# Expert rows of a two-block network: gate, diagonal and add of a row move into the row's own turn

## The chip, the cores and the metric

The kernel runs on one core of a Trainium2 chip. The metric is the device time of one launch in microseconds (us); lower is better. A core has five engines with instruction streams of their own that meet only at semaphores: TensorE (PE), VectorE (DVE), ScalarE (ACT), GpSimd (POOL), and SyncE (SP), which here only issues DMAs. Each stream is executed in its written order, so an instruction that waits holds up all that is written behind it on its engine.

## The reference

All data are float32: 512 tokens, width 1024. A first block (two layers: short convolution or state-space mixer, each with a gated feed-forward) is followed by a hybrid layer (band attention beside a gated delta rule) and then by the part that this change is about, a product-key retrieval of single-neuron experts. For each block of 128 tokens:

```
top_s, pos = lax.top_k(cand_s, 16)            # 8 heads x 16 = 128 experts per token
gates = softmax(top_s)
u, vv = expert_down[experts], expert_up[experts]
act = gelu(sum_d u * h)                       # one dot product per token and expert
out = sum_k (gates * act) * vv                # weighted sum of 128 rows of 1024
```

Every token needs 128 rows of two tables, 4 KB each: with 512 tokens that is 537 MB.

## The kernel before

**Chunks and rows.** The tokens are worked in four chunks `c` of 128, one token per partition. A "row" `n` = 128c + s (s from 0 to 127) is the s-th expert of all 128 tokens of chunk c at once. POOL gathers it (`pool_gather`, L2173) with one indirect DMA: 1 MB, 2048 words a partition, first the down half and then the up half. `GG` is 1, so a group is one row. The gathers go into a ring of buffers: 7 slots for rows 0 to 255, 12 from row 256 on. A gather waits until the row that used its slot before has been added (L2178).

**The work on one row** is: a dot product of the down half with the token's vector on DVE (`dve_dots`, L2182); the gelu of the 128 dots on ACT (L2200); the product with the row's gate; and the add of the up half, weighted by the result. Three rows of four (and for n of 256 and more 15 of 16) are added by PE: ACT makes a 128x128 diagonal matrix of the weights (`act_diag`, L2206), and PE multiplies it with the up half in two matmuls into two PSUM banks (`pe_add`, L2218). The others are DVE's own (`own_add`, L2163): s at least 24 and s = 1 mod 4 while n is below 256, s = 9 mod 16 after that. DVE adds such a row with one multiply-add of 1024 columns (`dve_add`, L2249). PE and ACT skip it.

**What runs between the rows.** The order of each engine's stream is written out by hand in `pe_experts` (L2306), `act_experts` (L2323) and `dve_experts` (L2342), which all loop over the 512 rows. In each odd row, every engine also does one step of other work (`steps_of`, L2297): for chunks 0 and 1 a step of `main`, the whole hybrid layer of the second half of the tokens (normalisation, projections, attention, the delta rule with its inversion `pe_invert`/`dve_invert`, output, queries), and beside it steps of the top-16 search of the next chunk (`dve_topk`, all on DVE). The step of an odd row is the same step on all three engines. In the inversion, the products of PE's step are masked or subtracted by DVE in the same step, and PE's next step needs the result.

**The order inside a row's turn `g`, before:**

- DVE: dots(g); gate product (g-1); own add (g-1), if it is DVE's; if g is odd, the step.
- ACT: gelu(g); diagonal(g-1); if g is odd, the step.
- PE: if g is odd, the step; add(g-1).

So the weight of a row passes ACT, DVE, ACT and PE, and its gate, diagonal and add stand in the turn of the row after it. L numbers in the profile are mostly those of helpers (`Engine`, L137 to L217): L153 is a matmul, L158 a transpose, L164 an ACT operation, L187 the dot product, L170 a tensor-tensor operation on DVE, L182 a multiply-add on DVE, L216 a gather.

Of the kernel before, what the change touches and what calls it, by code (L numbers as in the profile page):

```python
# [5 lines left out]
ALU = mybir.AluOpType  # L6
ACT = mybir.ActivationFunctionType
# [13 lines left out]
GG = 1  # L21
# [205 lines left out]
def build(nc, t, out):  # L227
    ctx = ExitStack()
    with ctx:
# [891 lines left out]
        t_at = [0]  # L1121

        def room(n):
            a = t_at[0]
            t_at[0] += n
            assert t_at[0] <= WORDS - LOW, t_at[0]
            return tail[:, a:a + n]
# [20 lines left out]
        gates = [room(128) for _ in range(2)]  # L1148
        eidx = [room(128).bitcast(U32) for _ in range(2)]
        dots = [room(GG) for _ in range(8)]  # L1150
# [3 lines left out]
        d_nega = room(1)  # L1154
        sm = [room(4) for _ in range(4)]
        NRING = (WORDS - LOW - t_at[0]) // 2048
        RING = t_at[0]
        ring_mem = [room(2048) for _ in range(NRING)]
        T = tiles(over[:, 4096:6144], 8)
        Sb = [over[:, 6144 + 512 * i:6656 + 512 * i] for i in range(3)]  # L1160
# [28 lines left out]
        k_dve, k_gate, idx_ok, gate_ok = [signal(n) for n in ("ranked", "gate_exp", "experts_found", "gates")]  # L1189
        tk_pe, f_pe, f_g, f_add = [signal(n) for n in ("turned_h", "turned_x", "gate_row", "out_added")]  # L1190
        g_dot, g_gelu, g_act, g_diag, g_mm = [
            signal(n) for n in ("dots", "gelu", "gated", "diag", "expert_added")]
# [959 lines left out]
        GROUPS = 128 // GG  # L2152
# [37 lines left out]
                e.wait_ge(*g_in.at((c, GG * grp + i)))  # L2190
                e.ttr(s[:, 0:1024], s[:, 0:1024], htk[c % 2], d[:, i:i + 1]).then_inc(*g_dot.tick(n + i))

        def dve_gate(e, c, grp):
            n = 128 * c + GG * grp
            d = dots[(n // GG) % 8]
            e.wait_ge(*g_gelu.at(n))
            e.wait_ge(*gate_ok.at(c))
            e.tt(d, d, gates[c % 2][:, GG * grp:GG * grp + GG], ALU.mult).then_inc(*g_act.tick((c, grp)))

        def act_gelu(e, c, grp):  # L2200
            n = 128 * c + GG * grp
            d = dots[(n // GG) % 8]
            e.wait_ge(*g_dot.at(n + GG - 1))
            e.act(d, d, ACT.Gelu).then_inc(*g_gelu.tick(n))

        def act_diag(e, c, grp):  # L2206
            n = 128 * c + GG * grp
            d = dots[(n // GG) % 8]
            e.wait_ge(*g_act.at((c, grp)))
            for i in range(GG):  # L2210
                if own_add(n + i):
                    continue
                k = turn[n + i]
                if k >= 8:
                    e.wait_ge(*g_mm.at(by_pe[k - 8]))
                e.act(diag[k % 8], ident, ACT.Copy, scale=d[:, i:i + 1]).then_inc(*g_diag.tick(n + i))

        def pe_add(e, c, grp):  # L2218
            for i in range(GG):
                s_i = GG * grp + i  # L2220
                n = 128 * c + s_i
                if own_add(n):
                    continue
                if s_i == 0:
                    for u in range(2):
                        ps.claim(("acc", c, u), (u,))
                        e.wait_ge(*ps.vacant(("acc", c, u)))
                e.wait_ge(*g_in.at((c, s_i)))
                e.wait_ge(*g_diag.at(n))
                for u in range(2):  # L2230
                    ins = e.mm(ps["acc", c, u], diag[turn[n] % 8], SLOTS[slot_no[n]][:, 1024 + 512 * u:1536 + 512 * u],
                               s_i == 0, s_i == 127)
                ins.then_inc(*g_mm.tick(n))

        def pe_finish(e, c):
            for u in range(2):
                o = ps.claim(("gB", c, u), HB)
                e.wait_ge(*ps.vacant(("gB", c, u)))
                e.wait_ge(*der_ok.at((5, "post")))
                for k in range(4):  # L2240
                    ins = e.mm(o[:, part[k]], post(5, 4 * u + k).broadcast_to([128, 128]), ident)
                ins.then_inc(*f_pe.tick(("gB", c, u)))
                o = ps.claim(("xo", c, u), HB)
                e.wait_ge(*ps.vacant(("xo", c, u)))
                for k in range(4):
                    ins = e.tr(o[:, part[k]], xT[:, 4 * u + k, 128 * c:128 * c + 128], ident)
                ins.then_inc(*f_pe.tick(("xo", c, u)))
# [56 lines left out]
        ALL_GROUPS = [(c, grp) for c in range(4) for grp in range(GROUPS)]  # L2304

        def pe_experts(e):  # L2306
            main = pe_main(e, 1)
            before_rows(main, iter(()))
            for g, (c, grp) in enumerate(ALL_GROUPS):
                if grp == 0:  # L2310
                    ranks = iter(()) if c == 3 else wait_steps(32)
                    late = pe_tok(e, 3) if c == 2 else iter(())
                if grp % 2:
                    steps_of(c, grp // 2, main, ranks)
                    next(late, None)
                if g:
                    pe_add(e, *ALL_GROUPS[g - 1])
                if g and grp == 0:
                    pe_finish(e, c - 1)
            pe_add(e, *ALL_GROUPS[-1])  # L2320
            pe_finish(e, 3)

        def act_experts(e):  # L2323
            ranked = [act_topk(e, c) for c in range(4)]
            main = act_main(e, 1, ranked[2])
            before_rows(main, iter(()))
            drive(ranked[0])
            for g, (c, grp) in enumerate(ALL_GROUPS):
                if grp == 0:
                    ranks = iter(()) if c == 3 else ranked[c + 1]  # L2330
                    late = act_tok(e, 3) if c == 2 else iter(())
                act_gelu(e, c, grp)
                if g:
                    act_diag(e, *ALL_GROUPS[g - 1])
                if c and grp == 8:
                    store(e, c - 1)
                if grp % 2:
                    steps_of(c, grp // 2, main, ranks)
                    next(late, None)
            act_diag(e, *ALL_GROUPS[-1])  # L2340

        def dve_experts(e, ranks):  # L2342
            ranked = [ranks] + [dve_topk(e, c) for c in range(1, 4)]
            main = dve_main(e, 1, ranked[2])
            before_rows(main, ranks)
            drive(ranks)
            for g, (c, grp) in enumerate(ALL_GROUPS):
                if grp == 0:
                    ranks = iter(()) if c == 3 else ranked[c + 1]
                    late = wait_steps(3) if c == 2 else iter(())  # L2350
                dve_dots(e, c, grp)
                if g:
                    dve_gate(e, *ALL_GROUPS[g - 1])
                    dve_add(e, *ALL_GROUPS[g - 1])
                if c and grp == 1:
                    dve_finish(e, c - 1)
                if grp % 2:
                    steps_of(c, grp // 2, main, ranks)
                    next(late, None)
            dve_gate(e, *ALL_GROUPS[-1])  # L2360
            dve_add(e, *ALL_GROUPS[-1])
            dve_finish(e, 3)

# [230 lines left out]
```

## Time and profile before

| | |
|---|---|
| time, median of 3 runs | 3613.56 us (3610.62 to 3616.09) |
| time of the profiled execution | 3612.0 us |
| its span in the profile | 3610.2 us |
| busy: PE / weight load / DVE / ACT / POOL | 3070.5 / 2105.5 / 2132.0 / 1193.7 / 603.5 us |
| first gather starts | 2100.9 us |
| gathers | 512, in 73728 packets, 536.90 MB |
| chain that ended last | PE 60%, DVE 16%, DMA 13%, ACT 5%, issue 4% |

The span is from the first instruction to the end of the last. An engine's busy time is the union of its instructions. The granted TensorE clock (PEclk) is a share of full speed. A row of the timeline has the start in us from the span's start, the duration in us, engine, line, operation, tiles (written<-read), shape, how many instructions were merged, and in brackets the idle time before it with what ended it. Rows of the kernel can be told by counting the dot products (L187 with 128x1024): the 91st is that of row 90.

### The profile page before, as it was taken

What the parts mean: (1) busy time and instruction counts of PE and PEld (TensorE: products, weight loads), DVE (VectorE), ACT (ScalarE), POOL (GpSimd) and SP (SyncE); (2) the same over time, 40 slices, a digit from 0 to 9 for tenths busy, and PEclk for the clock granted to TensorE, in tenths of its full rate; (3) what the DMA queues carried; (4) which work ended last, traced back from release to release, by engine and by line L of the source; (5) the groups of instructions that cost most, each with busy time, mean ns of one, the idle gap of its engine ahead of it and who ended that gap; (6) DMA issues with size and microseconds to landing.
All of it is one profiled execution on the core that took longest, in us unless ns stands there. A gap on an engine that the chain in (4) does not pass through costs nothing.

```text
span 3610.2 us, 34684 instructions
## 1 busy us (share of the span) xinstructions
PE 3070.5 (85%) x12138; PEld 2105.5 (58%) x12138; DVE 2132.0 (59%) x4304; ACT 1193.7 (33%) x2363; POOL 603.5 (17%) x540
## 2 busy tenths in 40 slices
PE   5989999798777989998998887988889677777777
PEld 4868888587565768886777753655457222222222
DVE  6655443676455454433353589876656978755555
ACT  2233222443444432222562345651222211211111
POOL 0000000000000000000000022323343454444442
PEclk9999999899888999999999998999999799999999
DMA  5534444242111324442311286988999899999997
GB/s 219 188 125 140 140 141 141 77 142 89 47 36 41 117 94 140 140 144 72 129 60 58 97 312 233 353 352 299 362 397 381 313 409 421 421 422 421 421 422 326
DMA packets 147548, 797.83 MB, mean 221 GB/s; under 512 B 16304, under 2 KB 18480, under 8 KB 81712
## 3 DMA queue, kind: packets, MB, share of 16 engines
q0 software_dynamic: 73728, 536.90, 37.2%
q1 hardware_dynamic: 69840, 251.69, 21.3%
q10 hardware_dynamic: 3808, 7.02, 0.5%
q8 instruction: 98, 1.61, 0.2%
q14 instruction: 74, 0.61, 0.0%
HBM read 793.46 MB, written 2.10 MB: 220 GB/s over the span
## 4 chain that ended last, share of the span: by engine, by line
PE 60%; DVE 16%; DMA 13%; ACT 5%; issue 4%; POOL 0%; DVEq 0%; SPq 0%; ACTq 0%
PE psum L153 60%; DMA tail<-in_experts,tail 13%; DVE tail L187 5%; ACT arena L164 3%; DVE tail L170 2%; DVE arena L182 2%; ACT L164 2%; DVE tail L182 1%; DVE tail L193 1%; DVE tail L190 1%; DVE region L170 1%; PE psum L158 1%; ACT region L164 1%; DVE tail L196 1%; DVE tail L205 1%
## 5 line engine op out<-in xcount | busy, mean ns | idle before, releaser
L153 PE MATMUL psum<-tail,arena 128*128 128x512 f32 (+2 forms) x3652 | 1322.9, 510 | 317.1 <-ACT arena L164 293.5
L153 PE MATMUL psum<-rounded,rounded 128*128 128x512 f32 x5496 | 1293.0, 396 | 40.9 <-DVE rounded L182 28.2
L153 PEld LDWEIGHTS psum<-tail,arena 128*128 128x128 f32 x3652 | 687.9, 199 | 903.0 <-issue 847.2
L153 PEld LDWEIGHTS psum<-rounded,rounded 128*128 128x128 f32 x5496 | 1036.2, 190 | 280.7 <-issue 56.1
L216 POOL DMA_INDIRECT tail<-in_experts,tail x512 | 583.4, 1139 | 1840.2 <-DVE tail L199 949.5
L187 DVE CUSTOM_DVE_ANT_0 tail<-tail 128x1024 f32<-128x1024 f32 x512 | 626.0, 1223 | 322.6 <-DMA tail<-in_experts,tail 320.2
L170 DVE TENSOR_TENSOR rounded<-arena,rounded 128x1024 fp32r<-128x1024 f32 (+2 forms) x285 | 316.3, 1110 | 346.7 <-ACT rounded L164 346.6
L164 ACT ACTIVATE tail<-tail 128x1 f32<-128x1 f32 (+2 forms) x544 | 115.4, 213 | 1032.5 <-DVE tail L187 878.0
L164 ACT ACTIVATE rounded<-arena 128x1024 fp32r<-128x1024 f32 (+2 forms) x317 | 291.9, 939 | 446.3 <-DVE arena L170 238.9
L153 PE MATMUL psum<-arena 128*128 128x1 f32 (+3 forms) x792 | 197.6, 374 | 75.1 <-ACT arena L164 45.2
L164 ACT ACTIVATE arena<-psum 128x256 f32<-128x256 f32 (+2 forms) x210 | 97.5, 480 | 440.3 <-PE psum L153 439.9
L164 ACT ACT_TABLE_LOAD x186 | 238.6, 1283 | 11.8 <-PE psum L153 6.4
L182 DVE SCALAR_TENSOR_TENSOR arena<-arena 128x512 f32<-128x512 f32 (+1 forms) x294 | 212.1, 724 | 21.8 <-ACT arena L164 10.9
L170 POOL TENSOR_TENSOR region<-region 128x256 f32<-128x256 f32 x24 | 19.9, 830 | 1131.0 <-DVE region L170 1131.0
L153 PEld LDWEIGHTS psum<-arena 128*128 128x128 f32 x792 | 127.3, 205 | 126.1 <-issue 81.0
L164 ACT ACTIVATE arena<-arena,tail 128x128 f32<-128x128 f32 x446 | 172.8, 388 | 0.8 <-issue 0.2
L170 DVE TENSOR_TENSOR tail<-tail 128x1 f32<-128x1 f32 (+4 forms) x555 | 134.4, 243 | 30.8 <-ACT tail L164 24.0
L153 PE MATMUL psum<-tail 128*128 128x128 f32 (+4 forms) x888 | 136.9, 300 | 16.8 <-DVE tail L182 14.7
L170 DVE TENSOR_TENSOR arena<-psum,arena 128x512 f32<-128x512 f32 (+1 forms) x88 | 41.5, 475 | 168.3 <-PE psum L153 168.0
L153 PEld LDWEIGHTS psum<-tail 128*128 128x128 f32 (+2 forms) x888 | 107.7, 185 | 52.5 <-issue 28.7
L182 DVE SCALAR_TENSOR_TENSOR arena<-psum,arena 128x511 f32<-128x511 f32 (+3 forms) x112 | 79.8, 712 | 77.0 <-ACT arena L164 44.0
L164 ACT ACTIVATE arena<-arena 128x512 f32<-128x512 f32 (+3 forms) x138 | 80.7, 598 | 89.9 <-DVE arena L170 29.3
(82 smaller groups left out, 1537.8 us busy)
## 6 DMA issues: line engine op xcount, KB each, us to landing
arena<-in_ada SPq DMA_DIRECT2D x136, 512.0 KB, 3.8
arena<-in_fin SPq DMA_DIRECT2D x88, 512.0 KB, 4.3
arena<-in_win SPq DMA_DIRECT2D x56, 512.0 KB, 3.3
arena<-in_fout SPq DMA_DIRECT2D x32, 512.0 KB, 4.1
arena<-in_mxbc SPq DMA_DIRECT2D x32, 512.0 KB, 4.1
arena<-in_pq SPq DMA_DIRECT2D x32, 512.0 KB, 5.2
arena<-in_ain SPq DMA_DIRECT2D x24, 512.0 KB, 4.7
arena<-in_mz SPq DMA_DIRECT2D x16, 512.0 KB, 3.6
```

The source lines that it names most:

```text
L153: return self.e.matmul(o, a, b, start=start, stop=stop, skip_group_check=skip)
L158: return self.e.transpose(o, a, ident)
L164: return self.e.activation(o, a, func, bias=bias, scale=scale)
L170: return self.e.tensor_tensor(o, a, b, op)
L182: return self.e.scalar_tensor_tensor(out=o, in0=a, scalar=s, in1=b, op0=op0, op1=op1)
L187: return self.e.tensor_tensor_reduce(o, a, b, 1.0, 0.0, ALU.mult, ALU.add, total)
L190: return Unissued() if self.e is None else self.e.max(o, a)
L193: return Unissued() if self.e is None else self.e.max_index(o, m, a)
L196: return Unissued() if self.e is None else self.e.match_replace(o, m, a, -3.0e38)
L205: return Unissued() if self.e is None else self.e.tensor_reduce(o, a, AX_X, op)
L216: return self.e.indirect_dma_start(out=o, out_offset=None, in_=table, in_offset=bass.IndirectOffsetOnAxis(ap=rows, axis=0))
```

## The change

The gate product moves from DVE to ACT, as a copy with a per-partition scale, right behind the gelu of the same row; ACT makes the diagonal in the same turn; PE adds the row in the same turn. DVE's own add stays one turn later. The order in turn `g` becomes:

- DVE: dots(g); own add (g-1); if g is odd, the step.
- ACT: gelu(g); gate product(g); diagonal(g); if g is odd, the step.
- PE: if g is odd, the step; add(g).

The closing work of a chunk on PE (`pe_finish`) moves to the end of turn 127 of that chunk. `RING = t_at[0]`, which nothing reads, is deleted.

```diff
-        def dve_gate(e, c, grp):
-            n = 128 * c + GG * grp
-            d = dots[(n // GG) % 8]
+        def act_gate(e, c, grp):
+            n = 128 * c + grp
+            d = dots[n % 8]
+            e.wait_ge(*g_dot.at(n))
+            e.act(d, d, ACT.Gelu).then_inc(*g_gelu.tick(n))
+            e.wait_ge(*gate_ok.at(c))
             e.wait_ge(*g_gelu.at(n))
-            e.wait_ge(*gate_ok.at(c))
-            e.tt(d, d, gates[c % 2][:, GG * grp:GG * grp + GG], ALU.mult).then_inc(*g_act.tick((c, grp)))
-
-        def act_gelu(e, c, grp):
-            ...
-            e.wait_ge(*g_dot.at(n + GG - 1))
-            e.act(d, d, ACT.Gelu).then_inc(*g_gelu.tick(n))
+            e.act(d, d, ACT.Copy, scale=gates[c % 2][:, grp:grp + 1]).then_inc(*g_act.tick((c, grp)))
@@ pe_experts
-                if g:
-                    pe_add(e, *ALL_GROUPS[g - 1])
-                if g and grp == 0:
-                    pe_finish(e, c - 1)
-            pe_add(e, *ALL_GROUPS[-1])
-            pe_finish(e, 3)
+                pe_add(e, c, grp)
+                if grp == GROUPS - 1:
+                    pe_finish(e, c)
@@ act_experts
-                act_gelu(e, c, grp)
-                if g:
-                    act_diag(e, *ALL_GROUPS[g - 1])
+                act_gate(e, c, grp)
+                act_diag(e, c, grp)
...
-            act_diag(e, *ALL_GROUPS[-1])
@@ dve_experts
                 if g:
-                    dve_gate(e, *ALL_GROUPS[g - 1])
                     dve_add(e, *ALL_GROUPS[g - 1])
...
-            dve_gate(e, *ALL_GROUPS[-1])
```

## Rows read from the trace of the kernel before

**Rows 1.** Windows: us, busy us (instructions) per engine, PEclk, DMA share, GB/s.
```profile
2293.00:2366.00 73.00, 72.74 (x280) 50.10 (x279) 60.27 (x155) 50.65 (x99) 21.78 (x22) 1.00 0.97 374
2398.00:2525.00 127.00, 100.90 (x487) 67.72 (x488) 87.05 (x169) 26.74 (x73) 41.23 (x34) 0.92 0.80 293
...
2688.00:2807.00 119.00, 118.20 (x503) 84.27 (x501) 79.41 (x218) 29.19 (x105) 43.82 (x37) 1.00 0.96 380
2807.00:2893.00 86.00, 49.09 (x74) 17.74 (x73) 81.95 (x198) 18.77 (x54) 36.12 (x25) 0.76 0.82 312
2950.00:3590.00 640.00, 479.97 (x1009) 177.09 (x1009) 411.29 (x997) 125.61 (x497) 270.93 (x252) 0.97 1.01 420
```

**Rows 2.** Waits from 2100 to 2900: us in total, times, longest us.
```profile
POOL tail L216 <- PE psum L153: 472.3, 165, 9.6
...
DVE tail L187 <- DMA tail<-in_experts,tail: 76.9, 58, 3.9
```

**Rows 3.** Waits from 2398 to 2525 (inversion of the delta rule).
```profile
DVE tail L170 <- PE psum L153: 31.6, 14, 4.8
PE psum L153 <- ACT arena L164: 26.4, 15, 4.0
```

**Rows 4.** Timeline of PE in the inversion, rows 88 to 92.
```profile
2442.59 1.89 PE L153 MATMUL psum<-tail,arena 128*128 128x512 f32 x4
2444.32 1.95 PE L153 MATMUL psum<-tail 128*128 128x128 f32 x16
2447.90 1.96 PE L153 MATMUL psum<-tail,arena 128*128 128x512 f32 x4 [1.63 <-ACT arena L164]
2450.24 1.96 PE L153 MATMUL psum<-tail,arena 128*128 128x512 f32 x4 [0.39 <-ACT arena L164]
2452.04 3.73 PE L153 MATMUL psum<-tail 128*128 128x128 f32 x32
```

**Rows 5.** Timeline of DVE in the same stretch, rows 90 to 94.
```profile
2443.40 1.22 DVE L187 CUSTOM_DVE_ANT_0 tail<-tail 128x1024 f32<-128x1024 f32 x1
...
2444.54 0.15 DVE L170 TENSOR_TENSOR tail<-tail 128x1 f32<-128x1 f32 x1
...
2447.15 1.28 DVE L170 TENSOR_TENSOR tail<-psum,tail 128x512 f32<-128x512 f32 x2
2448.35 1.21 DVE L187 CUSTOM_DVE_ANT_0 tail<-tail 128x1024 f32<-128x1024 f32 x1
...
2457.01 1.22 DVE L187 CUSTOM_DVE_ANT_0 tail<-tail 128x1024 f32<-128x1024 f32 x1
```

**Rows 6.** Timeline of ACT in the same stretch, rows 90 and 91.
```profile
2444.66 0.20 ACT L164 ACTIVATE tail<-tail 128x1 f32<-128x1 f32 x1 [6.23 <-DVE tail L187]
...
2447.36 0.39 ACT L164 ACTIVATE arena<-arena,tail 128x128 f32<-128x128 f32 x1
```

**Rows 7.** Timeline of ACT in the projections, row 51.
```profile
2303.70 0.36 ACT L164 ACTIVATE arena<-psum 128x256 f32<-128x256 f32 x1
...
2305.38 0.42 ACT L164 ACTIVATE tail<-tail 128x256 f32<-128x256 f32 x1
2305.82 0.42 ACT L164 ACTIVATE arena<-tail 128x256 f32<-128x256 f32 x1
```

**Rows 8.** Timelines of PE and ACT around row 70.
```profile
2365.68 7.49 PE L153 MATMUL psum<-tail,arena 128*128 128x256 f32 x30
2374.69 1.96 PE L153 MATMUL psum<-tail,arena 128*128 128x512 f32 x4 [1.51 <-ACT arena L164]
2378.50 3.68 PE L153 MATMUL psum<-tail,arena 128*128 128x512 f32 x12 [1.85 <-ACT arena L164]
...
2373.71 0.29 ACT L164 ACTIVATE tail<-tail 128x1 f32<-128x1 f32 x2
```

**Rows 9.** Timelines of ACT and PE at the end of the kernel.
```profile
3599.06 0.20 ACT L164 ACTIVATE tail<-tail 128x1 f32<-128x1 f32 x1 [1.97 <-DVE tail L187]
...
3603.21 1.05 PE L153 MATMUL psum<-arena 128*128 128x128 f32 x8
```

More of the change, by code:

```diff
@@ L1156, in build @@
         NRING = (WORDS - LOW - t_at[0]) // 2048
-        RING = t_at[0]
         ring_mem = [room(2048) for _ in range(NRING)]
@@ L2191, in dve_dots @@
                 e.ttr(s[:, 0:1024], s[:, 0:1024], htk[c % 2], d[:, i:i + 1]).then_inc(*g_dot.tick(n + i))
-        def dve_gate(e, c, grp):
-            n = 128 * c + GG * grp
-            d = dots[(n // GG) % 8]
-            e.wait_ge(*g_gelu.at(n))
-            e.wait_ge(*gate_ok.at(c))
-            e.tt(d, d, gates[c % 2][:, GG * grp:GG * grp + GG], ALU.mult).then_inc(*g_act.tick((c, grp)))
-        def act_gelu(e, c, grp):
-            n = 128 * c + GG * grp
-            d = dots[(n // GG) % 8]
-            e.wait_ge(*g_dot.at(n + GG - 1))
-            e.act(d, d, ACT.Gelu).then_inc(*g_gelu.tick(n))
+        def act_gate(e, c, grp):
[4 more added lines that the diff above has]
+            e.wait_ge(*gate_ok.at(c))
+            e.wait_ge(*g_gelu.at(n))
+            e.act(d, d, ACT.Copy, scale=gates[c % 2][:, grp:grp + 1]).then_inc(*g_act.tick((c, grp)))
         def act_diag(e, c, grp):
```

## The prediction, made blind

> **What bounds the kernel now.** I read the windows of the expert phase first. From 2950 to 3590 the DMA engines are taken whole: share 1.01, 420 GB/s, while PE is busy for 480 us of 640 and ACT for 126 [rows 1]. A gather is 1 MB, so a row costs 2.5 us there whatever the engines do. The end of the kernel is therefore the moment at which this DMA-bound stretch starts, plus a fixed amount of gathering; time is won or lost before it, from the first gather at 2100.9 to about 2893. There the reader is to see a different limit in each stretch. From 2293 to 2366 and from 2688 to 2807 PE is busy nearly throughout (72.7 of 73 us, 118.2 of 119). From 2807 to 2893, and from 2107 to 2202 in the same way, DVE is (82.0 of 86: the top-16 search). From 2398 to 2525, the inversion, nobody is: PE 101 and DVE 87 of 127 us, and the DMA engines carry only 293 GB/s [rows 1]. The waits say what this stretch is: DVE waits 31.6 us for PE, and PE 26.4 us for ACT's diagonal [rows 3]. It is a loop between engines, bound by latency. So I read its timeline next, engine by engine [rows 4 to 6].
>
> **One turn of that loop, before.** Its length is four rows, 2443.40 to 2457.01 = 13.61 us [rows 5]. Call the rows 90 to 93; row 89 and row 93 are DVE's own, which PE skips. After the step of row 89, PE does add(88) at 2442.59, whose diagonal is long there, and at once the step of row 91 at 2444.32, 16 matmul records for two token chunks [rows 4]. Meanwhile DVE is at dots(90), own add and dots(91), and when it comes to its own part of step 91 at 2447.15, PE's products lie ready and it waits for nothing [rows 5]. Only then does PE do add(90), 2447.90, and add(91), 2450.24, and the step of row 93 at 2452.04 [rows 4].
>
> **The change, part by part.**
>
> *Gate product to ACT.* It is a dependent ACT operation on one column. Its duration I take from the gelu, 0.20 us [rows 6]. An ACT operation that needs the one before starts 0.02 us after that one's end (2305.38 + 0.42, next at 2305.82) [rows 7]; so gelu to product is 0.23, and product to diagonal again 0.23: the diagonal starts 0.46 after the gelu. Before, the diagonal (of the row before) started 0.10 after the gelu (2447.36, behind a gelu of 0.20 whose record ends at 2447.46). ACT's chain grows by 0.36 per row. Bounds: 0.2, if the two pipeline as before, and 0.8, if each step takes the 0.44 of the wide pair [rows 7]. The Trainium skill ("ScalarE: Activation LUTs", Rules for kernel authors) wants a multiply on VectorE and budgets about 0.3 us for each ACTIVATE. No row shows a one-column product on ACT; by that figure the chain would be 0.6 and not 0.46, some 4 us more in the sum below.
>
> *Gate product off DVE.* It lasts 0.15 but starts before the dot product's end (2444.54, against 2443.40 + 1.22) and sticks out by 0.07 [rows 5]. That counts where DVE is the bound, in some 50 rows: 2 to 3 us, I take -2. Elsewhere it is worth nothing. It also removes a wait of DVE for ACT's gelu, but behind it DVE next needs ACT's output or a slot, so nothing again.
>
> *Add in its own turn, on PE.* This is the term that decides. The same three adds per four rows are done, but PE's step of row g now stands behind add(g-1) and no more behind add(g-2). For g = 1 mod 4 little changes: step 93 stood behind add(91), which needs the turn of dots(92) anyway; now it stands behind add(92), which needs the same dots. For g = 3 mod 4 it does: row 89 is DVE's own, so step 91 could start with add(88) done; now it must wait for row 90's whole chain. Worked out: gelu(90) is at 2444.66; the diagonal at 2445.12; diagonal to matmul is 0.54 (2447.36 to 2447.90) [rows 4, 6], so add(90) at 2445.66; an add holds PE for 1.73 (2442.59 to 2444.32), so step 91 at 2447.39 and not 2444.32. The first half of its products is there 1.05 us later, and DVE's part starts about 2448.5 and not 2447.15; its second half waits for PE's as well, so dots(92) comes at 2450.05 and not 2448.35: +1.70. Behind that, gelu(92) comes 1.26 after the start of its dots (as 2443.40 to 2444.66), add(92) 1.00 after that, and step 93 another 1.80 later (2450.24 to 2452.04), at 2454.1 and not 2452.04. One turn of the loop becomes 2.06 us longer, 15%. Hidden before was PE's step 91, by DVE's two dot products and own add; its cover is gone.
>
> The rows 90 to 113 hold six such turns: 12.4 us. Two more lie ahead of them in the stretch, and two behind it up to 2558, where the delta rule's advance runs; their steps are of other lengths, some half as long, and I take the 1.70 of the first part alone for each: 6.8. Both terms together lie between 12 (the first part without the second, in fewer turns) and 24.
>
> *A long ACT step.* Around row 70, ACT is in table loads until 2373.71 [rows 8]. Before, PE does step 71 in the meantime (until 2365.68 + 7.49 = 2373.17), then waits for diagonal(70) until 2374.69 and for diagonal(71) until 2378.50; 1.8 behind that, at 2380.3, step 73 begins [rows 8]. Now step 71 stands behind add(70), whose own chain ends at 2374.9: it starts near 2376.6 and ends, with 3.7 of matmuls (a step of 16 records there, an estimate from 7.49 for 30), near 2380.3. Add(71) takes it to 2382.1, and add(72) needs a gelu behind ACT's step 71, which itself now has its product later: step 73 begins near 2384.8. PE is busy for long behind that, so it stays: +4.5. Bounds 0 and 7.
>
> *Projections, 2293 to 2366.* ACT's evacuation of PE's product (2303.70) stands behind the diagonal [rows 7], and DVE waits for it. That loop takes 0.36 more in each of 11 steps: 4. PE is busy here too, so the cost lies between 0 (PE alone decides) and 8. I take 4, since both loops have the same length.
>
> *PE-bound 2688 to 2807.* PE runs behind ACT's diagonals, so whether it adds g or g-1 first changes nothing: 0, or 2 at the start.
>
> *DMA-bound rest.* A slot is freed about one row (2.5 us) earlier, but the DMA engines are full: 0. *The end.* Before, add(510) and add(511) both come behind gelu(511) at 3599.06, and the closing matmuls start at 3603.21 [rows 9]. Now only add(511) does: one add less (1.73) and 0.36 more: -1.4.
>
> **Sum:** 12.4 + 6.8 + 4.5 + 4 - 2 - 1.4 = 24.3 us. On the profiled execution's 3612.0 that is 3636.3, and 1.5 more for the median of the runs shown: 3637. The bounds of the terms give 3620 to 3662.
>
> **Rivals.**
>
> *The ring pays back (faster).* Of the time from 2100 to 2900 POOL spends 472 us in 165 waits for a slot that PE frees [rows 2]. Every slot now comes back a row earlier, with 7 slots in all. If the gathers are what holds DVE back there, its 76.9 us of waits for landings shrink; two thirds gone and no loss elsewhere gives 3612 - 51 = 3561. For it: POOL's waits are the longest in the profile. Against it: DVE waits for landings in 58 places only, 1.3 us each [rows 2], and in the inversion what it waits for is PE [rows 3]; from 2688 to 2807 PE is the busy one anyway [rows 1]. The Trainium skill ("Perfetto Trace Analysis", Identifying Performance Opportunities) says that the same gap repeating can mean too few buffers. POOL's gaps repeat so, and by that rule this rival would win; but what the rule speaks of is the engine that should be saturated, and in the inversion that is none.
>
> *A draw.* The slots won shorten the waits for landings around 2581 to 2807 by about the 24 us that the loops lose: 3613.
>
> *Every step pays.* If PE's order costs 2.06 per four rows in all of rows 35 to 207, the PE-bound stretches too, since PE then waits at each step for ACT behind DVE: 43 times 2.06 = 89, so 3612 + 89 - 3 = 3698. Against it: there the diagonals are several us ahead of PE.
>
> **Chances.** Forecast 0.62, the ring 0.13, a draw 0.11, every step 0.14. A difference of under 0.2% (7 us) can't be told from none. Faster is the ring, 0.13; the same is the draw, 0.11; slower is the rest, 0.76. The predicted time is 3637. The range reaches down to the draw and up half way to the third rival: 3609 to 3668.
>
> **What would show it.** Right: between 2398 and 2558 four rows take about 15.7 us and not 13.6; PE's waits for ACT's diagonal there grow, and stand in front of the short step; DVE's masking behind dots of g = 3 mod 4 gets a wait for PE of about 1.3 us. The gate shows as a second one-column ACT operation 0.23 behind the gelu. The stretch at 420 GB/s keeps its rate and starts some 26 us later. Wrong: if the inversion keeps its 13.6 us, PE's step doesn't hang on the row; if waits for landings fall by tens of us, the ring decides; and if the PE-bound stretches grow, the ACT chain does.

## The result, and the profile after

The changed kernel takes 3643.96 us (median of 4 runs, 3642.29 to 3646.46), the kernel before 3612.09 in the same comparison (4 runs, 3608.34 to 3616.09): a ratio of 1.0087, with a 95% interval of 1.0070 to 1.0104. Forecast were 3637 and slower. The profiled execution took 3642.49, its span is 3640.6.

First the windows of the changed kernel. The window of the inversion begins 17 us later than in [rows 1] and is 20 us longer; the columns are the same.

```profile
2415.00:2562.00 147.00, 103.31 (x482) 68.59 (x480) 82.77 (x130) 37.58 (x101) 43.41 (x33) 0.89 0.65 237
2980.00:3620.00 640.00, 483.45 (x1012) 177.63 (x1011) 394.77 (x747) 226.35 (x752) 265.03 (x254) 0.97 1.01 421
```

The last stretch is as full as before: 421 GB/s and 1.01 against 420 and 1.01 [rows 1]. Only ACT has more in it, 226 us for 126, and that costs nothing there. The inversion is emptier: PE is busy for 103 of 147 us, where it was 101 of 127, the DMA engines carry 237 GB/s for 293, and PE's granted clock is 0.89 for 0.92. The waits say who waits for whom (changed kernel, 2100 to 2900: us in total, times, longest):

```profile
POOL tail L216 <- PE psum L153: 400.1, 156, 10.3
...
PE psum L153 <- ACT arena L164: 145.7, 58, 7.5
...
DVE tail L170 <- PE psum L153: 64.8, 30, 5.4
DVE tail L187 <- DMA tail<-in_experts,tail: 45.9, 29, 5.6
```

DVE waits less for landings (45.9 us for 76.9 [rows 2]), and this is what the rival of the ring had foreseen in kind. But it waits 64.8 us for PE, and PE 145.7 for ACT's diagonal. The same two lines before:

```profile
PE psum L153 <- ACT arena L164: 117.1, 54, 7.1
...
DVE tail L170 <- PE psum L153: 34.2, 17, 4.8
```

Both grew by about 30 us, and the time, 3643.96, lies above the first two rivals (3561 and 3613). Where the waits for landings fell is the next thing to look at. None of it is in rows 90 to 113 of the inversion, where DVE waits for no landing before or after; nearly all is in rows 128 to 207. There (first the kernel before, 2558 to 2811, then the changed one, 2598 to 2849):

```profile
DVE tail L187 <- DMA tail<-in_experts,tail: 68.7, 51, 3.9
...
DVE arena L182 <- PE psum L153: 5.5, 4, 2.4
```

```profile
DVE tail L187 <- DMA tail<-in_experts,tail: 37.4, 26, 5.2
DVE arena L182 <- PE psum L153: 32.1, 8, 4.1
```

DVE waits 31 us less for landings and 27 us more for PE's products, and the rows take 1.3 us less. PE is busy for over 90% of this stretch in both kernels (232.7 of 253 us, 230.0 of 251), so the wait changed its name and little else.

Now the turn of the inversion that the prediction worked out, engine by engine, in the changed kernel (start us, duration us, then the instruction). DVE, rows 90 to 98:

```profile
2459.08 1.22 DVE L187 CUSTOM_DVE_ANT_0 tail<-tail 128x1024 f32<-128x1024 f32 x1
...
2464.40 0.69 DVE L170 TENSOR_TENSOR tail<-psum,tail 128x512 f32<-128x512 f32 x1 [1.75 <-PE psum L153]
...
2465.90 1.22 DVE L187 CUSTOM_DVE_ANT_0 tail<-tail 128x1024 f32<-128x1024 f32 x1
...
2472.05 1.28 DVE L170 TENSOR_TENSOR tail<-tail,psum 128x512 f32<-128x512 f32 x2 [3.78 <-PE psum L153]
...
2475.03 1.22 DVE L187 CUSTOM_DVE_ANT_0 tail<-tail 128x1024 f32<-128x1024 f32 x1
...
2492.37 1.22 DVE L187 CUSTOM_DVE_ANT_0 tail<-tail 128x1024 f32<-128x1024 f32 x1
```

ACT, row 90:

```profile
2460.40 0.53 ACT L164 ACTIVATE tail<-tail 128x1 f32<-128x1 f32 x2 [5.14 <-DVE tail L187]
2460.96 0.40 ACT L164 ACTIVATE arena<-arena,tail 128x128 f32<-128x128 f32 x1
```

PE, rows 90 to 94:

```profile
2461.51 1.96 PE L153 MATMUL psum<-tail,arena 128*128 128x512 f32 x4 [3.07 <-ACT arena L164]
2463.31 1.95 PE L153 MATMUL psum<-tail 128*128 128x128 f32 x16
2465.09 1.88 PE L153 MATMUL psum<-tail,arena 128*128 128x512 f32 x4
2468.27 1.96 PE L153 MATMUL psum<-tail,arena 128*128 128x512 f32 x4 [1.29 <-ACT arena L164]
2470.06 3.73 PE L153 MATMUL psum<-tail 128*128 128x128 f32 x32
2477.47 3.35 PE L153 MATMUL psum<-tail,arena 128*128 128x512 f32 x4 [3.67 <-ACT arena L164]
```

The reader is to see the order that was foreseen. Before, step 91 (16 records) stood at 0.92 behind the dot product of row 90 (2444.32 against 2443.40 [rows 4, 5]), and DVE found its products ready. Now it stands at 4.23 behind it (2463.31 against 2459.08), with PE idle for 3.07 us in front of add(90), and DVE waits 1.75 us where it waited for nothing. The turn is 2459.08 to 2475.03 = 15.95 us, where it was 13.61. The next turn, to 2492.37, is 17.34: its add at 2477.47 takes 3.35 us and not 1.96, and the whole difference is there (1.39 us).

**Where the time went.** Each row of the experts has one dot product on DVE, and they are counted off in the traces. The table gives the time between the starts of the dot products of the rows named (us, one profiled execution of each kernel; "start" is when row 0's begins). The lower lines are the experiments of the next section; each is introduced there.

```
kernel              start |  0-44  44-70  70-90 90-114 114-128 128-208 208-256 256-end | row 0 to end
before             2107.3 | 166.0   92.8   77.4   81.4    33.6   252.3   142.0   657.5 | 1502.9
before, again      2114.6 | 166.2   92.6   80.8   81.4    33.6   252.7   143.1   657.7 | 1508.1
changed            2114.9 | 161.0   95.2   88.1  102.5    36.8   251.0   137.1   654.2 | 1525.7
changed, again     2107.3 | 160.8   95.2   88.0  104.3    38.4   251.1   136.3   654.6 | 1528.7
e1_pe_late         2115.0 | 161.9   95.2   64.8   66.5    34.2   246.1   137.0   654.4 | 1460.0
e2_own_even        2103.5 | 165.4   95.7   78.8   80.5    33.6   245.2   141.8   654.6 | 1495.7
e3_fill            2115.0 | 161.3   95.2   87.8   94.6    36.7   251.9   137.6   653.5 | 1518.6
e4_gate_only       2109.0 | 160.7   95.5   83.3   80.8    32.8   253.3   142.2   655.7 | 1504.5
e5_defer2          2115.0 | 162.5   95.1   76.1   80.7    31.9   250.2   136.7   654.2 | 1487.6
e6_defer0          2107.1 | 163.0   95.3   74.5   78.9    32.5   248.6   136.7   654.5 | 1483.9
e7_two_late        2109.1 | 171.7  109.2   65.4   65.0    36.4   257.6   138.2   653.6 | 1497.0
e8_ring6           2103.1 | 169.0   93.8   81.5   79.3    35.6   261.4   148.0   659.1 | 1527.8
```

Of the changed kernel's loss, 21.1 us lie in rows 90 to 113 and 3.2 in the 14 behind them; rows 70 to 89 lose 10.7, rows 44 to 69 lose 2.4; rows 0 to 43 give 5.0 back, rows 128 to 207 1.3, rows 208 to 255 4.9, the rest 3.3.

### The profile page after: what moved, and what is told of

The parts are those of the page before. It is cut to its first block, busy times and chain, and to the rows that moved or that the text cites. A ratio compares the mean times of both kernels' runs of the same rounds, so it can differ in the third digit from the quotient of the medians.

```text
span 3640.6 us, 34668 instructions
## 1 busy us (share of the span) xinstructions
PE 3077.4 (85%) x12138; PEld 2110.5 (58%) x12138; DVE 2091.3 (57%) x3792; ACT 1392.2 (38%) x2875; POOL 594.1 (16%) x540
## 4 chain that ended last, share of the span: by engine, by line
PE 59%; DMA 16%; DVE 15%; ACT 6%; issue 3%; POOL 0%; DVEq 0%; SPq 0%; ACTq 0%; POOLq 0%
PE psum L153 58%; DMA tail<-in_experts,tail 15%; DVE tail L187 4%; ACT arena L164 2%; DVE arena L182 2%; ACT L164 2%; DVE tail L170 1%; ACT tail L164 1%; DVE tail L182 1%; DVE tail L193 1%; DVE tail L190 1%; DVE region L170 1%; PE psum L158 1%; ACT region L164 1%; DVE tail L196 1%
## 5 line engine op out<-in xcount | busy, mean ns | idle before, releaser
L153 PE MATMUL psum<-tail,arena 128*128 128x256 f32 (+2 forms) x3652 | 1324.7, 511 | 357.0 <-ACT arena L164 333.4
L216 POOL DMA_INDIRECT tail<-in_experts,tail x512 | 574.0, 1121 | 1872.3 <-DVE tail L199 949.5
L164 ACT ACTIVATE tail<-tail 128x1 f32<-128x1 f32 (+1 forms) x1056 | 266.1, 252 | 817.9 <-DVE tail L187 796.8
L182 DVE SCALAR_TENSOR_TENSOR arena<-arena 128x512 f32<-128x512 f32 (+1 forms) x294 | 212.3, 724 | 21.8 <-ACT arena L164 10.8
L153 PE MATMUL psum<-region 128*64 128x128 f32 (+2 forms) x560 | 85.5, 387 | 33.9 <-DVE region L170 32.9
```

The source lines that it names most:

```text
L153: return self.e.matmul(o, a, b, start=start, stop=stop, skip_group_check=skip)
L164: return self.e.activation(o, a, func, bias=bias, scale=scale)
L182: return self.e.scalar_tensor_tensor(out=o, in0=a, scalar=s, in1=b, op0=op0, op1=op1)
L216: return self.e.indirect_dma_start(out=o, out_offset=None, in_=table, in_offset=bass.IndirectOffsetOnAxis(ap=rows, axis=0))
```

## Experiments

The theory (1): PE's step of row g now stands behind add(g-1) and so behind the newest dot product; DVE's work no longer covers it. Rivals: (A) ACT's longer chain costs it, whatever PE's order; (B) a part of the loss lies ahead of row 0 and belongs to the code; (C) to add in the row's own turn costs at every step; the price of a slot is measured at the end. Beside them stands theory (2): the fall of PE's clock in the inversion is a price of its own. Edits are against the changed kernel where nothing else is said.

**PE's add one turn later again.** ACT still makes gelu, product and diagonal in the row's own turn.

```diff
-                pe_add(e, c, grp)
-                if grp == GROUPS - 1:
-                    pe_finish(e, c)
+                if g:
+                    pe_add(e, *ALL_GROUPS[g - 1])
+                if g and grp == 0:
+                    pe_finish(e, c - 1)
+            pe_add(e, *ALL_GROUPS[-1])
+            pe_finish(e, 3)
```

> The changed kernel, except that PE adds row g-1 in turn g, as before the change. ACT keeps gelu, gate product and diagonal in the row's own turn. Theory 1 (PE's step lost its cover: it now stands behind the add of the row just before it): the inversion goes back to about 13.6 us for four rows, without PE's 3.1 to 3.7 us waits ahead of those adds; what is left of the change is a gain of some 4 to 6 us on DVE's search stretches: 3605 to 3613, ratio to before 0.998 to 1.000. Rival A (ACT's chain of 0.56 us from gelu to diagonal, where it was 0.10, is what costs): stays at 3630 to 3644, since that chain is kept. Rival B (7.6 us of the difference lie ahead of the first row and belong to the code): they show again at row 0.

Measured: 3570.08 (5 runs, 3567.15 to 3578.18), 0.9883 of the kernel before (0.9867 to 0.9899; its median 3612.46). The order on PE is what costs, as theory 1 has it, and rival A falls. But the size was missed by some 35 us: this kernel is not level with the one before but 1.2% faster, the fastest of this study. The expectation had the inversion back at 13.6 us a turn; it went to 11.47. Its PE in the same stretch, rows 90 to 94, whose dots(90) starts at 2448.45 and dots(94) at 2459.92:

```profile
2448.76 1.95 PE L153 MATMUL psum<-tail 128*128 128x128 f32 x16
2450.88 1.96 PE L153 MATMUL psum<-tail,arena 128*128 128x512 f32 x4 [0.17 <-ACT arena L164]
2453.16 1.96 PE L153 MATMUL psum<-tail,arena 128*128 128x512 f32 x4 [0.32 <-ACT arena L164]
2454.95 3.73 PE L153 MATMUL psum<-tail 128*128 128x128 f32 x32
2458.52 1.88 PE L153 MATMUL psum<-tail,arena 128*128 128x512 f32 x4
```

Step 91 is back ahead of add(90), and add(90), which waited 1.63 us for its diagonal before [rows 4], waits 0.17. Before, diagonal(90) stood on ACT behind gelu(91), hence behind dots(91). Made at once, it lies ready, and step 93 starts 6.50 us behind dots(90) instead of 8.64 (2452.04 less 2443.40 [rows 4, 5]). The turn is 11.47 us. So the change joins a gain with a larger loss. Of DVE's waits from 2100 to 2900, that for landings is longer here than in the kernel before (76.9 us [rows 2]), though the kernel is the fastest:

```profile
DVE tail L187 <- DMA tail<-in_experts,tail: 91.4, 68, 5.9
```

**The gate's product alone.** The edit of e1, and on ACT also the diagonal one turn later: only the product has moved, from DVE to ACT.

```diff
-                act_diag(e, c, grp)
+                if g:
+                    act_diag(e, *ALL_GROUPS[g - 1])
+            act_diag(e, *ALL_GROUPS[-1])
```

> The gate product moves to ACT, but ACT's diagonal and PE's add stay one turn later as in the kernel before. Theory 1: no step loses its cover; DVE is rid of 512 small operations: 3604 to 3611 (ratio 0.998 to 1.000), about as the kernel with only PE's add late. Rival A (the second ACT operation itself costs): some us slower than before, the more in the projections (2293 to 2366), 3620 or more.

Measured: 3614.95, a ratio of 1.0007 (0.9997 to 1.0017): no difference. It was expected at 3604 to 3611, a little faster, with 3620 or more as the rival (A); it falls between the two. It gains 5.3 us in rows 0 to 43, where DVE is the bound, and loses 2.7 in rows 44 to 69. This and the kernel of e1 differ only in the turn in which ACT makes the diagonal: 3614.95 - 3570.08 = 45 us. And e1 and the changed kernel differ only in the turn of PE's add: 3643.96 - 3570.08 = 74 us the other way. 3 - 45 + 74 is the whole result. (These are differences of medians of several batches; in the profiled executions, from row 0 to the end, the two are 44.5 and 65.7 us.) The 45 us do not come from the inversion alone: rows 70 to 89 give 18.5 of them, rows 90 to 113 14.3, rows 128 to 255 12.4.

**DVE's own rows laid on even turns.** The rows that DVE adds itself become n = 2 mod 4 instead of 1 mod 4, so PE has no row to add just ahead of its step of n = 3 mod 4.

```diff
-            return s >= 24 and (s % 4 == 1 if n < 256 else s % 16 == 9)
+            return s >= 24 and (s % 4 == 2 if n < 256 else s % 16 == 10)
```

> The changed kernel, except that DVE's own rows are s = 2 mod 4 (and 10 mod 16) and not 1 and 9. The work is the same. Theory 1: PE has now nothing to do between add(1) and the step of row 3, so this step no longer stands behind the row just before it; its cover is back though each add stays in its own turn: four rows of the inversion take 13.6 to 14.1 us, in all 3606 to 3620. Rival A (ACT's longer chain): nothing changes, 3640. Rival C (adding in the row's own turn costs at every step): the inversion stays above 16 us, 3635 or more.

Measured: 3607.85, 0.9987 (0.9979 to 0.9996), 36 us under the changed kernel, with its ACT chain kept and every add still in its own turn. So neither (A) nor (C) costs what the changed kernel loses. Rows 90 to 113 take 80.5. Its turn is 13.82 us (dots(90) 2443.40, dots(94) 2457.22). In the turn behind it PE idles 1.31 and 1.52 us ahead of its two adds, not 3.67 as in the changed kernel:

```profile
2457.53 1.95 PE L153 MATMUL psum<-tail 128*128 128x128 f32 x16
2460.79 1.96 PE L153 MATMUL psum<-tail,arena 128*128 128x512 f32 x4 [1.31 <-ACT arena L164]
2464.27 1.96 PE L153 MATMUL psum<-tail,arena 128*128 128x512 f32 x4 [1.52 <-ACT arena L164]
```

The cost sits where an add of a new row stands ahead of a step, as theory 1 says.

**Which of the two steps.** Two kernels put one of the two adds of a turn of four behind the step that follows it: e5 with k = 2 (the add of n = 2 mod 4 goes behind step n = 3 mod 4), e6 with k = 0 (that of n = 0 mod 4 behind step n = 1 mod 4). The edit is shown once for both.

```diff
+                if grp % 4 == k + 1: pe_add(e, c, grp - 1)     # behind the step
...
-                pe_add(e, c, grp)
+                if grp % 4 != k: pe_add(e, c, grp)
```

> The changed kernel, but PE's adds of rows n = 2 mod 4 come behind the step of the next row, so that only this step (rows n = 3 mod 4) is freed from the row just before it; the step of rows n = 1 mod 4 still stands behind add(n-1). By my prediction this is the whole loss: the inversion goes to about 14 us for four rows, rows 90 to 114 to 83 us (working from the timeline of the kernel with late adds: dots, gelu, gate and diagonal put step 93 2.4 us later than its 11.5 us loop has it). Rival (each kind of step costs half): 88 to 94.

> The opposite half: PE's adds of rows n = 0 mod 4 come behind the next step (n = 1 mod 4), the step of rows n = 3 mod 4 stays behind add(n-1). If a half can be taken alone, as I work it out from the timeline of the kernel with late adds, the loop takes about 12.8 us and rows 90 to 114 take 77 us. By my prediction, which gave all the loss to the other kind of step, it stays near 100.

Measured: e5 3602.18, 0.9966 (0.9949 to 0.9982); e6 3592.86, 0.9960 (0.9946 to 0.9973). Rows 90 to 113 take 102.5 with neither step freed, 80.7 with step 3 alone, 78.9 with step 1 alone and 66.5 with both (e1). The prediction said that step 3 is what the change costs and that step 1 stands as before. e5 bears this out: with step 3 free and step 1 still behind the newest row the stretch is back at 80.7, where it was 81.4. e6 does not: by the prediction it was to stay near 100, and it went to 78.9. Each step costs something behind a new row, and more when the other one stands there too: step 3 costs 12.4 us with step 1 free (66.5 to 78.9) and 21.8 with step 1 bound (80.7 to 102.5); slow adds, the subject of the next experiment, are a part of both. What is true of the prediction's claim is that the kernel before had paid for step 1 already, since its diagonal was made so late, and not for step 3. (The medians of e5 and e6 lie 9 us apart, but the intervals of their ratios overlap.) DVE in e5, rows 90 to 94:

```profile
2448.64 1.22 DVE L187 CUSTOM_DVE_ANT_0 tail<-tail 128x1024 f32<-128x1024 f32 x1
...
2452.12 1.28 DVE L170 TENSOR_TENSOR tail<-psum,tail 128x512 f32<-128x512 f32 x2
...
2459.50 1.29 DVE L170 TENSOR_TENSOR tail<-tail,psum 128x512 f32<-128x512 f32 x2 [3.78 <-PE psum L153]
...
2462.49 1.22 DVE L187 CUSTOM_DVE_ANT_0 tail<-tail 128x1024 f32<-128x1024 f32 x1
```

The masking of step 91 waits for nothing again, that of step 93 for 3.78 us, and the turn is 13.85. The kernel before waited 3.17 us at that place, and e1 takes it down to 1.40: its adds of rows 90 and 91 hardly wait for their diagonals (0.17 and 0.32 us, above). DVE, first the kernel before, then e1:

```profile
2454.02 1.28 DVE L170 TENSOR_TENSOR tail<-tail,psum 128x512 f32<-128x512 f32 x2 [3.17 <-PE psum L153]
```

```profile
2456.93 1.29 DVE L170 TENSOR_TENSOR tail<-tail,psum 128x512 f32<-128x512 f32 x2 [1.40 <-PE psum L153]
```

**Filling PE's idle time.** The slow add of the changed kernel at 2477.47 can be laid beside the clock that PE was granted (window 2477 to 2479; the columns are those of the windows, so the clock is the 0.50):

```profile
2477.00:2479.00 2.00, 1.53 (x2) 0.84 (x3) 1.60 (x3) 0.65 (x3) 1.27 (x1) 0.50 0.05 20
```

It is half of full speed, the lower of the two levels; over the turn before, 2459 to 2475, it is 1.00. The experiment asks whether PE's activity decides it. In rows 88 to 115, at n = 2 mod 4, PE does two more matmuls with a zero stationary matrix before it waits for the diagonal. They add zero to the sums; only PE's activity changes.

```diff
+            if 88 <= n < 116 and n % 4 == 2:
+                for u in range(2):
+                    e.mm(ps["acc", c, u], zero, SLOTS[...][:, 1024+512*u:1536+512*u], False, False)
             e.wait_ge(*g_diag.at(n))
```

> The changed kernel, and for rows 88 to 115 with n = 2 mod 4 PE does two more matmuls of 128x512 with a zero matrix (they add nothing) before it waits for the diagonal, in time in which it stands idle. Theory 2 (in the inversion the adds of 3.0 to 3.8 us behind an idle time of 3.67 us are slow because the granted clock fell; others take 1.96): the idle time is cut to about 1.9 us, the adds take 1.96, a turn falls from 17.3-17.9 to about 15.9 us, 6 to 10 us less in all: 3634 to 3638. Rival (these adds are slow because of the data or the memory they read): they stay at 3.3, and the time at 3644.

Measured: 3628.94, 1.0046 (1.0033 to 1.0058). Rows 90 to 113 go from 102.5 to 94.6. The add at the place of the slow one, PE of this kernel:

```profile
2477.45 1.99 PE L153 MATMUL psum<-tail,arena 128*128 128x512 f32 x4 [1.86 <-ACT arena L164]
2479.27 1.95 PE L153 MATMUL psum<-tail 128*128 128x128 f32 x16
```

It takes 1.99 us again and not 3.35, though PE was given more to do. Of the five such adds (rows 94 to 110) four take 1.99; one, that of row 98, still takes 3.21. The median fell by 15 us, more than the 6 to 10 that were expected. In the profiled executions, from row 0 to the end, it is 7.1 us, and this is the number that belongs to the filled stretch. Turn by turn, from row 90 on (us between the starts of the dot products of rows 90, 94, ... 114, read off the traces):

```
before       13.61  14.67  14.62  13.62  13.61  11.23
changed      15.95  17.34  18.85  17.62  17.65  15.08
e3_fill      15.89  15.89  17.57  15.89  15.89  13.52
e1_pe_late   11.47  11.48  11.48  11.48  11.48   9.09
changed, 2nd 15.95  18.97  17.62  17.65  17.51  16.56
e8_ring6     13.61  13.61  13.62  13.61  13.61  11.23
```

The reader is to see a base and something on top. Without the slow adds the six turns would be 5 x 13.61 + 11.23 = 79.3 us before and 5 x 15.89 + 13.52 = 93.0 after: 13.7 us for the wait. The slow adds put 2.1 on top before (two turns of six) and 9.5 after (five of six): 7.4 us for the clock. The two make the 21.1. The last line, the kernel before with one slot less (below), happens to have no slow add here, and it takes those 79.3 us. How often the clock falls is not fixed: in its second profile the changed kernel takes 104.3 us and not 102.5, so the clock's part is 7 to 9 us.

**Both kernels again.** No edit; one more profile of each.

> The kernel before, unchanged, for a second profile. In the first pair of profiles the changed kernel reaches row 0 7.6 us later than the kernel before, though all code ahead is the same; nearly all of it arises between 870 and 1000 us. If this offset is a matter of the single execution, this profile lies somewhere between the two (row 0 at 2103 to 2115 us); if it belongs to the kernel, row 0 is at 2107.3 again.

> The changed kernel, unchanged, on the chip of this batch, for a second profile and its ratio beside the others. Row 0 at 2114.9 again if the offset ahead of the rows belongs to the kernel, otherwise anywhere from 2103 to 2115. The stretch of rows 90 to 114 takes 102.5 us again, ratio to before 1.007 to 1.010.

Measured: the kernel before 3624.5 in that one execution (span 3622.7), the changed one 3639.79 (5 runs, 3637.8 to 3646.58), 1.0087 (1.0074 to 1.0101). The start of row 0 moves by 7.3 us between two executions of the same kernel, 2107.3 and 2114.6 for the one, 2107.3 and 2114.9 for the other. A reader who took the 7.6 us between the first two profiles for a cost of the change ahead of the experts would have been wrong: rival (B) gets nothing from these profiles. From row 0 to the end the two kernels differ by 17.6 to 25.8 us, 21.7 in the mean, which is less than the 30 to 32 of the medians. These 8 to 10 us stay open. A hint: the one execution of the kernel before with the late start, 3624.5, lies above its 11 others (3607 to 3621), and the one of the changed kernel with the early start, 3637.8, is the lowest of its five. So the changed kernel may have the late start more often. Executions without a profile don't show where row 0 begins, so this is not shown. The second profile missed its expectation for rows 90 to 113 a little, 104.3 for 102.5.

**Three rows held back.** PE keeps up to three rows in hand in rows 24 to 119 of the first two token blocks of 128, so that no step waits for a new row; ACT as in the changed kernel.

```diff
+                held.append((c, grp))
+                while len(held) > (3 if c < 2 and 24 <= grp < 120 else 1):
+                    pe_add(e, *held.pop(0))
```

> As the kernel with PE's add one turn late, but in rows 24 to 119 of the first two chunks PE holds three rows back instead of one, so a step never stands behind a row of its own pair; in exchange each of the seven slots is held longer. Theory 1: in the inversion only the engines' own work is left, PE 10.6 us per four rows (three adds of 1.73, steps of 1.8 and 3.6), so rows 90 to 114 take 63 to 65 us instead of 66.5; elsewhere little. Rival (slots): with slots coming back later DVE waits for landings in the stretches near the DMA limit and the gain is eaten or turned: rows 128 to 208 take over 250 us instead of 246, the total above 3572.

Measured: 3603.16 (9 runs), 0.9982 (0.9969 to 0.9996). The inversion is as fast as hoped, 65.0, but rows 44 to 69 take 109.2 for 95.2, rows 0 to 43 9.8 more than in e1, rows 128 to 207 11.5 more. DVE waits for landings in 91 places, by this line of its waits from 2100 to 2900 (e1: 68 places, 91.4 us):

```profile
DVE tail L187 <- DMA tail<-in_experts,tail: 131.1, 91, 5.5
```

The rival was right. The added waits for landings are about the added time, stretch by stretch: 13.1 us for e1's 3.5 in rows 0 to 43, 17.2 for 2.7 in rows 44 to 69. Rows held back are up to three slots of seven that no gather can use, and they cost more than the last microsecond of the loop brings.

**The kernel before, with one slot less.**

```diff
+        NRING -= 1
```

> The kernel before with a ring of 6 slots instead of 7 (11 instead of 12 from row 256 on). This prices a slot, and so the rival by which slots that come back a row earlier pay for the change. If the gathers hold DVE back before row 256, one slot fewer costs some 15 to 40 us. By my prediction they don't: 0 to 8 us slower, with the inversion (rows 90 to 114) at 81 us as it was.

Measured: 3640.20 (4 runs), 1.0085 (1.0070 to 1.0100): 30 us for one slot (22 in the mean from row 0 to the end of the profiled executions), where 0 to 8 were expected. Its waits from 2100 to 2900:

```profile
POOL tail L216 <- PE psum L153: 487.0, 168, 9.5
...
DVE tail L187 <- DMA tail<-in_experts,tail: 113.8, 78, 5.6
```

POOL's wait hardly moved, 487.0 for 472.3 [rows 2]; DVE's for landings went from 76.9 to 113.8 us, which is of the size of the loss. It is a price only between kernels whose engines are otherwise as fast: e1 waits 91.4 us for landings and is 42 us faster than the kernel before. The loss is spread: 9 us in rows 128 to 207, 5 to 6 in rows 208 to 255, 3 in rows 0 to 43; the inversion lost nothing (79.3). The slots were worth more than the prediction gave them, outside the stretch on which it had fixed its eye.

## Why the prediction was right, and where its sizes were off

*Right, and shown: the step that lost its cover.* The place of PE's add is the cause: put back one turn it gives the whole loss back and more (e1), and with step 3 alone freed the inversion is where it was (e5). ACT's longer chain costs little (the 2.4 us of the projections, and a turn of 13.85 in e5 for 13.61), and the gate alone changes nothing in sum (e4). Wrong was the side remark that for step 1 "little changes": freeing step 1 alone saves as much as freeing step 3 (e6, 78.9, where the prediction's reading gave about 100). The clockwork held as well: dots(90) to dots(92) was forecast at 6.65 us and is 6.82, dots(92) to step 93 4.05 and 4.16, step 93 to dots(94) 4.97 and 4.97. The turn is 15.95, forecast 15.67. What is missing is small and known: the diagonal starts 0.56 behind the gelu and not 0.46, twice a turn, and the gelu 0.06 later.

*Mis-sized: the term of the inversion, 12.4 forecast, 21.1 measured.* The forecast priced the wait alone, and this was 13.7. It took PE's durations from one turn [rows 4], where each add lasts 1.96 at the most. In all five adds of the changed kernel behind 3.67 us of idle time (rows 94, 98, 102, 106, 110) the add took 3.02 to 3.75 us, nearly the double at the most, as the level of 1.2 GHz gives against that of 2.4; the granted clock at the first of them is 0.50. The other 7.4 us are this, and e3, which fills the idle time, gets 7.9 back: shown. The PEclk of 0.92 in [rows 1] could have warned: two turns of six had such an add before the change. With the rows behind (3.4 forecast, 3.2 measured) this part was right.

*Row 70 and the turns up to 90: 4.5 and 3.4 forecast, 6.7 and 4.0 measured.* PE, changed kernel:

```profile
2367.75 5.41 PE L153 MATMUL psum<-tail,arena 128*128 128x512 f32 x20 [0.56 <-ACT arena L164]
2379.89 5.42 PE L153 MATMUL psum<-tail,arena 128*128 128x512 f32 x9 [6.73 <-ACT arena L164]
```

Where PE did step 71 during ACT's table loads and then waited 1.51 and 1.85 us [rows 8], it now stands for 6.73 in one piece. The mechanism is the one that was named.

*Projections: 4 forecast, 2.4 measured.* Every kernel with the product on ACT has 95.1 to 95.7 there (but for e7, which holds rows back), so it is the product, whatever PE does.

*DVE without the gate: -2 forecast, -5 measured,* all of it in rows 0 to 43, by e4. The forecast had counted only the 0.07 us by which it sticks out of a dot product, in 50 rows. At 44 rows, 5.3 us are 0.12 each. Between two dot products with nothing but the gate between them it is 0.10: their starts are 1.23 us apart before (2155.76 and 2156.99) and 1.13 in e4 (2156.06 and 2157.19). The rest is not shown. Nor is it shown why rows 208 to 255, where the prediction also took DVE for the bound, gain nothing in e4 (142.2 for 142.0).

*Slots that come back earlier: 0 forecast,* and rows 128 to 255 gave 6.2 back. e8 shows what a slot is worth, about 30 us, so the rival of the ring had something in it: DVE's waits for landings did fall, by 31 us. But they fell in rows 128 to 207, where DVE then waited for PE in their place; in the inversion, where the time was lost, there were none to win. How the 6.2 come about is open: e1 gains in rows 128 to 207 (6.2) and in rows 208 to 255 (5.0), e2 only in the first, the changed kernel mostly in the second.

*End: -1.4 forecast, -1.3 measured* (from the last dot product, 12.4 to 11.1). *DMA-bound rest: 0 forecast, -2.0 measured.*

**The sum.** 24.3 were forecast; the terms of the table add up to 22.8 (1525.7 - 1502.9), on the medians 31.9. So the total agrees partly by luck, because errors cancel: 11.5 us too little from row 70 to row 113, some 11 us of gains not seen. Two slips of the prediction's own sums change nothing: 3636.3 and 1.5 are 3638 and not 3637, and its bounds give 3650 or so at the top; 3662 needs ACT's chain at 0.8 us as well.

**What the prediction did not see** is no term of its sum but the halves of one. It compared the order before with the order after, and in that balance the diagonal made at once seemed worth nothing, since PE's next step took its place. Done alone it is worth 45 us (e4 against e1). It asked what the earlier product is spent on; it did not ask what it is worth if it is not spent.

## What to carry to other kernels

Where one engine makes something small for another, try to make it as early as its inputs allow and to use it a turn later: the two halves of such a change have prices of their own (here -45 and +74 us), and each is to be worked out alone. On an engine that works in order, see to it that a step of a loop between engines does not stand behind the newest row of another loop; here one row of distance was enough, and three cost more in slots than they won. The version that follows, e1, is the fastest, 3570 us.

A wait that shrinks is not yet time won: the longest waits of the profile (POOL's for slots) hardly moved with a slot less, and DVE's for landings gave way to a wait for PE. Compare the same rows in both kernels, not the waits alone.

## What the hardware showed that was not expected

The granted clock is part of a wait's price: the stretch of the inversion has 0.89 after and 0.92 before [rows 1], and with it go the adds of 3.0 to 3.8 us behind 3.67 us of idle time. What PE did before the fall: in the kernel before it had stood idle for 2.23 us only, ahead of the slow adds at 2461.51 and 2476.18, and three later adds behind the same 2.23 us took 1.96. So the idle time right in front does not decide alone, as PE of e6 shows, where the same idle time stands ahead of a slow add and of one at full speed:

```profile
2455.05 3.38 PE L153 MATMUL psum<-tail,arena 128*128 128x512 f32 x4 [1.95 <-ACT arena L164]
...
2469.44 1.96 PE L153 MATMUL psum<-tail,arena 128*128 128x512 f32 x4 [1.95 <-ACT arena L164]
```

And a program with the same instructions differs in length ahead of the experts, here by 7.3 and 7.6 us (the starts in the table lie anywhere from 2103.1 to 2115.0). Windows from 870 to 1000 us, first the kernel before in its first execution, then in its second:

```profile
870.00:1000.00 130.00, 93.94 (x544) 74.34 (x545) 67.25 (x132) 50.54 (x82) 9.58 (x12) 0.83 0.11 33
```

```profile
870.00:1000.00 130.00, 93.76 (x506) 73.57 (x506) 65.35 (x126) 50.27 (x81) 9.58 (x12) 0.77 0.11 33
```

PE is busy for the same time but gets through 38 matmuls less, at a granted clock of 0.77 for 0.83; the changed kernel has both starts too. Two profiles are therefore compared from a common mark behind such a stretch, not from the span's start.
